# Weight units of the half products shifted by 64 bytes in wider slots; six narrow tiles merged

## The reference

```python
x = x + rms_norm(mix, attn_post_norm)
h = rms_norm(x, ffn_pre_norm)
f = (silu(h @ w_gate) * (h @ w_up)) @ w_down
x = x + rms_norm(f, ffn_post_norm)        # three such layers, with three mixers
```

## Time and profile before

| | |
|---|---|
| median of 3 runs | 1867.03 us (1864.97 to 1872.48) |
| the profiled execution | 1873.32 us, its span 1871.1 us |
| mean granted TensorE clock | 0.988 |
| TensorE matmul busy | 1833.7 us, 98% |
| GpSimd busy | 1240.3 us, 66% |
| VectorE busy | 810.9 us, 43% |
| ScalarE busy | 430.2 us, 23% |

### The profile page before, as it was taken

The page is one execution under the profiler, slowest core; times in us unless marked ns, Lnnn a source line. Parts: engine busy times, 40 slices in busy tenths (PEclk is TensorE's granted clock), DMA queues, the critical chain, the costliest instruction groups (busy, mean ns, idle before and its releaser), DMA issues.

```text
span 1871.1 us, 25590 instructions
## 1 busy us (share of the span) xinstructions
PE 1833.7 (98%) x9410; PEld 1521.5 (81%) x9410; DVE 810.9 (43%) x1365; ACT 430.2 (23%) x880; POOL 1240.3 (66%) x743
## 2 busy tenths in 40 slices
PE   9999999999999999999999999999999999999997
PEld 7886678888888898777888888889878888888886
DVE  5355754533441045254554333005993463344103
ACT  4335672311110022131311111003334331111000
POOL 7975546866676558665876667667666686667652
PEclk9999999999999999999999999999998999999998
DMA  5431002233333214211232333222323223233311
GB/s 201 135 119 51 13 1 79 91 100 99 92 116 104 95 46 158 79 57 57 91 113 90 101 97 124 101 72 68 102 66 92 79 91 100 91 101 111 109 62 46
DMA packets 44877, 168.27 MB, mean 90 GB/s; under 512 B 4984, under 2 KB 7288, under 8 KB 44672
## 3 DMA queue, kind: packets, MB, share of 16 engines
q1 hardware_dynamic: 44496, 164.56, 27.6%
q10 hardware_dynamic: 304, 2.64, 0.4%
HBM read 165.07 MB, written 2.11 MB: 89 GB/s over the span
## 4 chain that ended last, share of the span: by engine, by line
PE 90%; DVE 4%; POOL 3%; issue 2%; ACT 1%; DMA 0%; POOLq 0%; SPq 0%; DVEq 0%
PE psum L584 27%; PE psum L586 26%; PE psum L585 26%; PE psum L802 2%; PE psum L786 1%; POOL w_lo L471 1%; DVE h_lo L1557 1%; DVE tmp L1599 1%; PE psum L828 1%; PE psum L634 1%; POOL w_hi L468 1%; PE psum L825 1%; PE psum L918 1%; PE psum L932 1%; POOL x L492 1%
## 5 line engine op out<-in xcount | busy, mean ns | idle before, releaser
L471 POOL TENSOR_TENSOR w_lo<-raw,w_hi 128x1024 fp32r<-128x1024 f32 (+1 forms) x286 | 747.9, 2615 | 23.9
L584 PE MATMUL psum<-h_hi,w_hi 128*128 128x512 f32 (+1 forms) x1744 | 657.7, 377 | 13.0 <-POOL w_lo L471 6.6
L586 PE MATMUL psum<-h_hi,w_lo 128*128 128x512 f32 (+1 forms) x1744 | 651.1, 373 | 0.0
L585 PE MATMUL psum<-h_lo,w_hi 128*128 128x512 f32 (+1 forms) x1744 | 650.9, 373 | 0.0
L468 POOL TENSOR_SCALAR w_hi<-raw 128x1024 fp32r<-128x1024 f32 (+1 forms) x286 | 324.3, 1134 | 444.9 <-PE psum L586 419.2
L584 PEld LDWEIGHTS psum<-h_hi,w_hi 128*128 128x128 f32 x1744 | 329.1, 189 | 81.2 <-issue 16.0
L586 PEld LDWEIGHTS psum<-h_hi,w_lo 128*128 128x128 f32 x1744 | 329.0, 189 | 58.4
L585 PEld LDWEIGHTS psum<-h_lo,w_hi 128*128 128x128 f32 x1744 | 329.2, 189 | 56.3 <-issue 0.2
L584 PE MATMUL psum<-g_hi,w_hi 128*128 128x512 f32 (+1 forms) x594 | 217.5, 366 | 0.0
L585 PE MATMUL psum<-g_lo,w_hi 128*128 128x512 f32 (+1 forms) x594 | 217.1, 365 | 0.0
L586 PE MATMUL psum<-g_hi,w_lo 128*128 128x512 f32 (+1 forms) x594 | 217.0, 365 | 0.0
(11 more groups left out here) (282 smaller groups left out, 1882.2 us busy)
## 6 DMA issues: line engine op xcount, KB each, us to landing
raw<-in_wide SPq DMA_DIRECT2D x239, 512.0 KB, 3.5
raw<-in_down SPq DMA_DIRECT2D x48, 704.0 KB, 4.0
decay<-decay_rows ACTq DMA_DIRECT2D x1, 2048.0 KB, 7.8
out<-x SPq DMA_DIRECT2D x16, 128.0 KB, 1.7
x<-in_xt SPq DMA_DIRECT2D x3, 512.0 KB, 6.9
x<-in_xt ACTq DMA_DIRECT2D x1, 512.0 KB, 4.6
angles<-in_angles SPq DMA_DIRECT2D x1, 512.0 KB, 10.3
cols<-in_cols SPq DMA_DIRECT2D x1, 221.0 KB, 4.4
```

The lines of the kernel that those rows point to most:

```text
L471: nc.gpsimd.tensor_tensor(w_lo[:, slot, 0:w], raw[:, j % RAW, 0:w], w_hi[:, slot, 0:w].bitcast(F32), ALU.subtract).then_inc(units_split, 1)
L584: pe.matmul(out_ap, lhs[0], rhs[0], start=first, stop=False)
L585: pe.matmul(out_ap, lhs[0], rhs[1], start=False, stop=False)
L586: return pe.matmul(out_ap, lhs[1], rhs[0], start=False, stop=last)
```

## The change

The units whose products go by halves form the set `BY_HALVES`: for each norm at unit `at` the units at-1, at, at+1 and at+2, and at-2 where the norm follows a w_down. For them GpSimd writes and TensorE reads the tiles 16 elements (64 bytes) further into the slot. Slots of `w_hi` and `w_lo` get 32 elements (128 bytes) more. GpSimd's loops cover four units with constant addresses, so the shifted units are taken out of them: `lead` at the beginning of a stretch, `tail` at its end. Six narrow tiles become parts of one, and the filler before `h_hi` goes from 64 to 32 bytes. `h_hi` and all behind it start 896 bytes later.

```diff
+BY_HALVES = frozenset(at + u for at in NORMS_AT for u in (-1, 0, 1, 2)) | {at - 2 for at in NORMS_AT if at not in NORMS_AT[::2]}
+ODD = 16
+
+
+def unit_place(j):
+    return ODD if j in BY_HALVES else 0
...
-        w_hi = sb("w_hi", [P, SLOTS, DOWN_UNIT * P], F32R)
-        w_lo = sb("w_lo", [P, SLOTS, DOWN_UNIT * P], F32R)
+        w_hi = sb("w_hi", [P, SLOTS, DOWN_UNIT * P + 2 * ODD], F32R)
+        w_lo = sb("w_lo", [P, SLOTS, DOWN_UNIT * P + 2 * ODD], F32R)
...
-        variance = sb("variance", [P, NB])
-        root = sb("root", [P, NB])
-        scale_col = sb("scale_col", [P, NB])
...
-        spare = sb("spare", [P, 1])
...
-        lam = sb("lam", [P, 8])
-        subln_s = sb("subln_s", [P, 1])
+        narrow = sb("narrow", [P, 24])
+        lam, variance, root, scale_col = narrow[:, 0:8], narrow[:, 8:8 + NB], narrow[:, 12:12 + NB], narrow[:, 16:16 + NB]
+        spare, subln_s = narrow[:, 20:21], narrow[:, 21:22]
...
-        sb("in_front_of_h", [P, 16])
+        sb("in_front_of_h", [P, 8])
...
-            def split(tiles, j):
+            def split(tiles, j, at=0):
                 slot, w = j % SLOTS, tiles * P
+                place = slice(at, at + w)
...
-                nc.gpsimd.tensor_scalar(w_hi[:, slot, 0:w], raw[:, j % RAW, 0:w], 1.0, 1.0, ALU.mult, ALU.mult)\
+                nc.gpsimd.tensor_scalar(w_hi[:, slot, place], raw[:, j % RAW, 0:w], 1.0, 1.0, ALU.mult, ALU.mult)\
...
-                nc.gpsimd.tensor_tensor(w_lo[:, slot, 0:w], raw[:, j % RAW, 0:w], w_hi[:, slot, 0:w].bitcast(F32),
+                nc.gpsimd.tensor_tensor(w_lo[:, slot, place], raw[:, j % RAW, 0:w], w_hi[:, slot, place].bitcast(F32),
...
-                times, rest = divmod(count - peel, SLOTS)
                 phase = n.base.get("units", 0)
+                lead = sum(j in BY_HALVES for j in range(phase, min(phase + TOGETHER, end)))
+                for j in range(lead):
+                    split(tiles, phase + j, unit_place(phase + j))
+                phase += lead
+                tail = sum(j in BY_HALVES for j in range(phase, end))
+                times, rest = divmod(end - phase - tail, SLOTS)
+                rest += tail
...
-                for j in range(rest):
-                    split(tiles, phase + j)
+                for j in range(end - rest, end):
+                    split(tiles, j, unit_place(j))
...
             def next_unit():
-                slot = n.base.get("units_split", 0) % SLOTS
+                j = n.base.get("units_split", 0)
+                slot, at = j % SLOTS, unit_place(j)
                 pe.wait_ge(units_split, n.take("units_split"))
-                return [lambda t, w=w: w[:, slot, t * P:(t + 1) * P] for w in (w_hi, w_lo)]
+                return [lambda t, w=w: w[:, slot, at + t * P:at + (t + 1) * P] for w in (w_hi, w_lo)]
```

## The result

The changed kernel is slower: median 1886.41 us (1884.46 to 1887.2, five runs) against 1864.97 (1864.72 to 1872.48), ratio 1.0082 with a 95% interval of 1.0063 to 1.0100. The forecast of 1864.9 (1858 to 1873) was wrong, and it named the wrong side. The profiled execution took 1887.1 us, its span 1885.3; before, the span was 1871.1.

The account below looks back on a forecast made before the run. TensorE, busy 98% of the span, was taken to bound the kernel. From 1867.0, quicker half products gave -2.1 us, new distances, tmp and written-out splits 0: 1864.9 us, range 1858 to 1873.

Parts of the forecast that it names:

- What bounds the kernel: Whole kernel: TensorE bounds it, busy 98% of the span, against GpSimd 66% and VectorE 43%.
- the 13 ns on top of the columns: TensorE steps: 13 ns above the columns' own time, in full (226.8) and half (120.0) products, dependent on weight load against stream.
- four half products of 117.5 ns each: Behind the statistics products, 316.36 to 316.83: steps quicker than 120 ns, read as showing the extra 13 ns vary.
- The depthwise rows: Full products with tokens at every element offset: 232.3 ns each, 5.5 above aligned ones; taken as a high bound.
- The 64 bytes: Shifted weights of 1260 half products: 116 ns instead of 120, 522 of them on the path, -2.1 us.
- Which products are on the path: Half products: 522 of 1260 count; 693 in openings are hidden behind GpSimd's split, 15 more behind each w_out.
- Wider slots, merged narrow tiles: 5802 full products under new distances modulo 256: 0 taken; each nanosecond would weigh 5.8 us.
- I take 0, by the latter: Price of new distances for full products, put at 0 because the 280-column rows showed no difference.
- the 280-column products: Products reading the weight slot at 0, 96 and 64 bytes past a multiple of 128: 128 and 129 ns, no difference.
- the full products pay: Rival, chance 0.11: moving h_hi and g tiles by 896 bytes slows 5802 full products; at 3 ns +17.4 - 2.1, 1882.
- Written-out splits, tmp: GpSimd's splits taken out of loops, same instructions: 0; tmp's new place, read by adds to x: 0, 4 us either way possible.

Follow-up runs that it names:

- layout_only: The changed kernel with a shift of 0 for the half units, all else kept; ratio to the kernel before 1.0083.
- the version by slots: The changed kernel with unshifted units in slots 0 and 2 written and read 128 bytes further; ratio to the kernel before 0.9981.
- fix_no_shift: The version by slots with the 64 bytes taken out, every product 0 bytes apart modulo 256; ratio to the kernel before 0.9996.
- h_64_later: The kernel before with the filler in front of h_hi 64 bytes larger and nothing else; single run, 1879.92 us.

## Why the prediction was wrong

*What bounds the kernel, and that the 13 ns on top of the columns are no constant*: right. Full products take 226.7 to 233.3 ns at one clock, by address alone, and half ones 113.4 to 120. But the row that the prediction leaned on, four half products of 117.5 ns each, doesn't show it. With the step ahead of them, which starts here,

```profile
316.23 0.28 PE L584 MATMUL psum<-h_hi,w_hi 128*128 128x256 f32 x1
```

it is five steps in 0.60 us up to 316.83, 120.0 ns each. The four look quick only because a slow one stands before them. The depthwise rows were the real evidence; on this one the inference came right by luck.

*The 64 bytes*: right in sign and near in size. 116 ns was forecast; the rows at the ends of stages have 113.4 to 117.8, those of the openings 114 to 116. That 116 is close is luck in part: it was the middle between today's pace and the load's, and the runs have two levels, 113.4 and 117.8, on either side of it. The forecast of 2.1 us for this part stands against 1.7 us (the changed kernel against `layout_only`) and 1.1 us (the version by slots against `fix_no_shift`), both without the first part and the Conformer's. The Trainium skill, "TensorE: Matmul & The Clock Gate", section "Step-by-step: what each phase is for", has two independent read ports and so 0 for this part; by that rule neither full nor half products would answer to a distance, and here both do (226.7 against 232.5 ns, 119.9 against 113.4 to 117.8), so the trace doesn't agree.

*Which products are on the path*: right. The idle time behind an opening rose from 0.46 to 1.03 us, that is, the quicker openings only wait longer, and leaving the openings unshifted changed nothing.

*Wider slots, merged narrow tiles*: here it failed, in the term of the full products under their new distances, with the words "I take 0, by the latter". The distance modulo 256 had been named as what changes, and what each nanosecond weighs had been worked out, but its price was taken from the 280-column products, which turn out to be deaf to it. The depthwise rows, +5.5 ns, were the better witness: 232.3 there, 232.5 to 233.3 measured at distances other than 0 and 64. At 6 ns in two slots of four that is 3 ns a product, 17.4 us, less 2.1: 1882.3, the figure that the rival "the full products pay" gave for 3 ns. Spans say +14.2, the ratio +15.3. What made 280 columns seem nearest was that their offsets came closest to the edit; what should have spoken against them is that their steps never run as evenly as those that were to be priced (226 or 227, thousands of times). A steady pace at one alignment shows what this alignment gives, and nothing of its neighbours. The rival got 0.11; with the one aligned layout in the whole kernel and no row at another distance, it deserved far more. Of the things that came with the edit, only the distance counts: the wider slots, the merged tiles and the new place of h_hi by themselves cost nothing (`fix_no_shift`).

*Written-out splits, tmp*: right, 0 (`fix_no_shift`).

## What to carry to other kernels

When a change moves buffers that TensorE reads, compare for every pair of stationary operand (the weights) and moving operand (the tokens) the distance modulo 256 bytes before and after, not just modulo 128, and slot by slot where slots rotate: a width that is an odd multiple of 128 puts every other slot out of step. If thousands of products run at one even pace, treat their alignment as something that was won and can be lost, and price the loss by the products that run unaligned. A gain of 2 to 6 ns on some hundred products is worth having only if the other six thousand keep their place. The figures are those of one shape, 512 columns with a load of 128; another shape must be run (the 280-column products show no effect).

## What the runs showed of the hardware that was not expected

The step of a product of 512 columns with a load of 128, both operands fp32r (F32R in the kernel), depends on where the two operands stand to each other: 226.7 ns at distance 0 modulo 256 bytes, 228.9, 232.5 and 233.3 elsewhere. Modulo 512 nothing changes: in the version by slots the distance is 256 modulo 512 in slots 0 and 1 and 0 in slots 2 and 3, and all four run at 226.7. Why the chip answers to this distance no run here shows. For products of 256 columns distance 0 is the slowest, 119.9 ns.

The step of the half products is not settled by the distance alone. The last two units of the stream (285 and 286, the end of the last w_down) have the same half-product addresses in the changed kernel and in the version by slots, and step at 113.4 and 117.8 ns; the full products just ahead stand otherwise. But that is not what decides it either: in `h_64_later` every product, full or half, has the same distance, and the same 98 steps at the end of the second w_down and of the third go at different paces. The second:

```profile
1264.79 0.28 PE L584 MATMUL psum<-g_hi,w_hi 128*128 128x256 f32 x1
...
1276.33 0.28 PE L586 MATMUL psum<-g_hi,w_lo 128*128 128x256 f32 x1
```

11.54 us, 117.8 ns each; and the third:

```profile
1847.54 0.28 PE L584 MATMUL psum<-g_hi,w_hi 128*128 128x256 f32 x1
...
1858.65 0.28 PE L586 MATMUL psum<-g_hi,w_lo 128*128 128x256 f32 x1
```

11.11 us, 113.4 ns each. Each pace is held over all 98 steps. What chooses it is open; it was not tried.

In the attention stage TensorE waits for other engines, and the clock granted there differs from one profiled execution to another. Even `fix_no_shift`, whose products keep the paces of the kernel before, took 3.0 us less than it up to the first start, and no other part of it differs by more than 0.13 us. Span, busy time with records, granted clock, DMA share and GB/s from 170 to 210 us, before:

```profile
170.00:210.00 40.00, 35.43 (x288) 0.87 0.09 28
```

and in the version by slots:

```profile
170.00:210.00 40.00, 36.52 (x332) 1.00 0.05 15
```

In the first, part of the stage ran at the lower level of 1.2 GHz, in the second all of it at 2.4 GHz.
